# Experts in an order worked out on the chip: by fours at 64 rows, by eights at 32

## The reference

```python
N_GROUPS, EXPERTS_PER_GROUP, TOP_E, D_EXPERT = 4, 8, 2, 512        # 32 experts
def hier_moe(h, wr_g, br_g, wr_e, br_e, w_gate, w_up, w_down):
    p_group = softmax(xf @ wr_g + br_g)
    p_top, g_sel = top_k(p_group, 1)                               # one group of eight
    fine = (xf @ wr_e + br_e)[of that group]
    e_val, e_sel = top_k(fine, 2)                                  # two experts in it
    gate = p_top * softmax(e_val)
    ...
        return (silu(xb @ w_gate[e]) * (xb @ w_up[e])) @ w_down[e] # 1024->512, 1024->512, 512->1024
    out[token] += gate * that
```

## Time and profile before

| | |
|---|---|
| median of three runs | 2012.52 us (2011.01 to 2013.88) |
| span of the profiled execution | 2011.5 us (its own time is not listed apart from the three) |
| PE busy | 1958.3 us, 97% |
| DVE busy | 1026.8 us, 51% |
| first expert stage, router's logits to first addition of its result | 861 to 1331 us |
| second expert stage, the same | 1531 to 1998 us |
| transfers | 593 MB, mean 295 GB/s |

### The profile page before, as it was taken

The page is one execution under the profiler, slowest core; times in us unless marked ns, Lnnn a source line. Parts: engine busy times, 40 slices in busy tenths (PEclk is TensorE's granted clock), DMA queues, the critical chain, the costliest instruction groups (busy, mean ns, idle before and its releaser), DMA issues.

```text
span 2011.5 us, 21703 instructions
## 1 busy us (share of the span) xinstructions
PE 1958.3 (97%) x8110; PEld 1084.0 (54%) x8110; DVE 1026.8 (51%) x1940; ACT 375.6 (19%) x783; POOL 122.8 (6%) x217
## 2 busy tenths in 40 slices
PE   8999999999999999899999999989999999999997
PEld 5557666545776658454444434447865444344442
DVE  3356875445597669686668796743444111011102
ACT  2421001033110000131111111112332211111111
POOL 1121210011121100000000000000000000000000
PEclk9999999999999999899999999999999999999999
DMA  7437876334587751669999999973254999999995
GB/s 264 154 126 256 303 288 251 132 126 167 204 285 287 279 209 43 254 265 408 426 428 427 427 426 427 427 294 126 84 196 173 408 428 427 426 427 427 425 428 235
DMA packets 113351, 593.14 MB, mean 295 GB/s; under 512 B 17767, under 2 KB 22374, under 8 KB 85990
## 3 DMA queue, kind: packets, MB, share of 16 engines
q1 hardware_dynamic: 99430, 541.48, 67.0%
q0 software_dynamic: 13824, 50.34, 7.1%
HBM read 590.74 MB, written 1.05 MB: 294 GB/s over the span
## 4 chain that ended last, share of the span: by engine, by line
PE 87%; DVE 7%; issue 2%; DMA 1%; POOL 1%; ACT 1%; DVEq 0%; SPq 0%; POOLq 0%; ACTq 0%
PE bank L1251 28%; PE bank L897 11%; PE bank L910 10%; PE bank L1124 7%; PE bank L829 6%; PE bank L1226 5%; PE bank L1242 4%; DVE work L2689 3%; PE bank L1034 3%; PE bank L1144 3%; PE bank L943 1%; PE bank L1394 1%; DMA ring<-in_moe_w_up 1%; PE bank L1234 1%; POOL rstd L749 1%
## 5 line engine op out<-in xcount | busy, mean ns | idle before, releaser
L1251 PE MATMUL bank<-ring,work 128*64 128x512 f32 x2240 | 632.7, 593 | 1.5 <-DMA ring<-in_moe_w_up 1.5
L1251 PEld LDWEIGHTS bank<-ring,work 128*64 128x64 f32 x2240 | 202.1, 137 | 311.5 <-issue 311.4
L2689 DVE SCALAR_TENSOR_TENSOR work<-work 128x512 f32<-128x512 f32 x384 | 262.0, 746 | 6.7 <-DVE work L2687 5.3
L897 PE MATMUL bank<-hT,ring 128*128 128x256 f32 x1024 | 225.1, 379 | 0.7 <-ACT hT L1551 0.7
L897 PEld LDWEIGHTS bank<-hT,ring 128*128 128x128 f32 x1024 | 194.4, 190 | 36.9 <-issue 11.7
L2699 DVE SCALAR_TENSOR_TENSOR work<-work,bank 128x512 f32<-128x512 f32 x32 | 22.0, 687 | 355.1 <-ACT work L1756 355.1
L1251 PE MATMUL bank<-seventh,work 128*64 128x512 f32 x384 | 169.1, 593 | 0.0
L1251 PE MATMUL bank<-work 128*64 128x512 f32 x312 | 140.3, 594 | 0.0
L1124 PE MATMUL bank<-hT,ring 128*128 128x256 f32 x608 | 137.9, 389 | 0.6 <-ACT hT L1666 0.6
L829 PE MATMUL bank<-ring,hT 128*128 128x512 f32 (+1 forms) x320 | 135.0, 579 | 0.0
L1124 PEld LDWEIGHTS bank<-hT,ring 128*128 128x128 f32 x608 | 117.9, 195 | 19.7 <-issue 3.2
(11 more groups left out here) (408 smaller groups left out, 2096.8 us busy)
## 6 DMA issues: line engine op xcount, KB each, us to landing
ring<-in_moe_w_gate SPq DMA_DIRECT2D x51, 2048.0 KB, 16.5
ring<-in_moe_w_down SPq DMA_DIRECT2D x44, 2048.0 KB, 19.8
ring<-in_moe_w_up SPq DMA_DIRECT2D x43, 2048.0 KB, 18.7
ring<-in_w_down SPq DMA_DIRECT2D x16, 2048.0 KB, 11.7
ring<-in_w_up SPq DMA_DIRECT2D x16, 2048.0 KB, 10.6
xn<-in_ada_w POOLq DMA_DIRECT2D x48, 512.0 KB, 6.4
work<-in_ada_w POOLq DMA_DIRECT2D x48, 512.0 KB, 7.4
ring<-in_w_in SPq DMA_DIRECT2D x10, 2048.0 KB, 8.1
```

The lines of the kernel that those rows point to most:

```text
L897: last = pe.matmul(b[:, (c % 2) * S:(c % 2) * S + S], w[:, k, c * P:c * P + P], hT[:, k, :], start=(k == 0), stop=(k == DT - 1))
L1251: last = pe.matmul(b[h, :], x[:, k, h], rows_of(i, j + e, k)[:, c0:c0 + 512], start=(k == 0), stop=(k == kk - 1))
L2689: mo.do(dve.scalar_tensor_tensor(fl(bias[:, h]), mask_b, rbt[:, bass.ds(12 * bk + h, 1)], fl(bias[:, h]), ALU.mult, ALU.add))
```

## The change

The order of the experts is worked out on the chip. Places 0 to 3 (`FIXED`) hold experts 0 to 3. Of experts 4 to 31 those with more than 32 tokens come first, then the others, each in their numbers' order. Places 0 to 15 (`HEAVY`) are done as before, in pairs at 64 rows. Places 16 to 31 are done four to a "pair", at 32 rows each (`LIGHT`), eight to a quad: there are 8 + 4 = 12 pairs and 6 quads. If more than 16 places are heavy, four passes are made.

A light pair's units are g, g, g, g, u, u, u, u, d, d, d, d. VectorE moves the ranks and gates into the new order (`rk_at`, `gg_at`) and writes the list of experts as integers (`order_i`). SyncE waits for `order_ready` and loads the number of each expert from place 4 on, when it comes to its gate matrix, and takes the source address of its three transfers from it. The last four units are split in halves, all first halves ahead of all second ones. The bias steps are spread over six quads instead of eight. The scratch for descriptors of POOL's transfers is given as 4096 bytes of a partition (it was not given before; the default is 16384).

```diff
+FIXED, HEAVY, LIGHT = 4, 16, 32
-        UNITS = 6 * (NE // 2)
-        WIDE_QUADS = 5
-        WIDE = 12 * WIDE_QUADS
-        NARROW = tuple(RING_OF[0][(WIDE + x) % 8] for x in range(8) if RING_OF[0][(WIDE + x) % 8] != 8)
+        UNITS = 3 * NE
+        HEAVY_PAIRS, HEAVY_UNITS = HEAVY // 2, 3 * HEAVY
+        PAIRS = HEAVY_PAIRS + (NE - HEAVY) // 4
+        QUADS = PAIRS // 2
+        WIDE = 60
+        NARROW = (5, 0, 1, 2, 3, 4, 6)
...
+            def moe_src(i, j):
+
+                e = place_of(j)
+                if e < FIXED:
+                    return moe_w[kind_of(j)][i, e]
+                if kind_of(j) == 0:
+                    sp.wait_ge(sM["order_ready"], i + 1)
+                    expert_at[e] = sp.value_load(order_i[i][0:1, e:e + 1], min_val=0, max_val=NE - 1)
+                src = moe_w[kind_of(j)][i]
+                return src[bass.ds(expert_at[e], 1), :, :, :].rearrange("e p k n -> (e p) k n")
...
+            def moe_second_halves(i):
+
+                for j in range(UNITS - 4, UNITS):
+                    rows = SLOT[slot_of(i, j)][0].rearrange("p (k n) -> p k n", k=4)
+                    sp.dma_start(rows[:, 2:4, :], moe_src(i, j)[:, 2:4, :]).then_inc(landed2[i], 16)
...
-                def product(b, x, j, k, kk, c0):
-
-                    for e in range(2):
-                        h = slice(SLOTS * e, SLOTS * e + SLOTS)
-                        last = pe.matmul(b[h, :], x[:, k, h], rows_of(i, j + e, k)[:, c0:c0 + 512], start=(k == 0), stop=(k == kk - 1))
+                def product(b, x, p, kind, k, kk, c0):
+
+                    ne, width, unit = shape_of(p)
+                    for e in range(ne):
+                        h = slice(width * e, width * e + width)
+                        last = pe.matmul(b[h, :], x[:, k, h], rows_of(i, unit + ne * kind + e, k)[:, c0:c0 + 512], start=(k == 0), stop=(k == kk - 1))
                     return last
...
                 do(dve.tensor_scalar(slotp, slot_no[:, :], 1.0, None, ALU.add))
+                do(dve.tensor_scalar(slotp_l, slot_no[:, 0:LIGHT], 1.0, None, ALU.add))
                 do(dve.tensor_copy(bcmp, bno))
+                do(dve.memset(over[:, 0:FIXED], 0.5))
...
                 do(dve.tensor_reduce(passes_f[:, 0:1], B(4)[:, 0:NE], AX_X, ALU.max))
+                do(dve.tensor_scalar(over[:, FIXED:NE], B(4)[:, FIXED:NE], float(LIGHT), 0.5, ALU.is_gt, ALU.mult))
...
-                do(dve.tensor_reduce(passes_f[:, 4:5], passes_f[:, 1:4], AX_X, ALU.add))
-                wait()
-                dve.tensor_scalar(passes_i[i][:, :], passes_f[0:1, 4:5], 1.0, None, ALU.add).then_inc(m["passes_ready"], 1)
+                do(dve.tensor_tensor_scan(count_up, over, over, 0.0, ALU.add, ALU.add))
+                wait()
+                do(dve.tensor_scalar(passes_f[:, 4:5], count_up[:, NE - 1:NE], float(HEAVY), 3.0, ALU.is_gt, ALU.mult))
+                wait()
+                do(dve.tensor_reduce(passes_f[:, 5:6], passes_f[:, 1:5], AX_X, ALU.add))
+                wait()
+                do(dve.tensor_scalar(passes_f[:, 6:7], passes_f[:, 5:6], 1.0, 4.0, ALU.add, ALU.min))
+                wait()
+                dve.tensor_copy(passes_i[i][:, :], passes_f[0:1, 6:7]).then_inc(m["passes_ready"], 1)
...
                 do(dve.tensor_tensor(gg[:, :, :], oh1[:, :, :], oh2[:, :, :], ALU.add))
-                wait()
+
+                do(dve.scalar_tensor_tensor(place_f, bcmp, count_up[:, NE - 1:NE], count_up, ALU.add, ALU.subtract))
+                wait()
+                do(dve.scalar_tensor_tensor(place, count_up, -1.0, place_f, ALU.add, ALU.subtract))
+                wait()
+                do(dve.scalar_tensor_tensor(place, over, 2.0, place, ALU.mult, ALU.mult))
+                wait()
+                do(dve.tensor_tensor(place, place, place_f, ALU.add))
+                wait()
+                do(dve.tensor_copy(rk_at[:, :, 0:FIXED], rk[:, :, 0:FIXED]))
+                do(dve.tensor_copy(gg_at[:, :, 0:FIXED], gg[:, :, 0:FIXED]))
+
+                def moved(dst, src):
+                    do(dve.tensor_tensor(perm_x, perm_eq, spread(src, 1, 14), ALU.mult))
+                    wait()
+                    do(dve.tensor_reduce(dst, perm_x, AX_X, ALU.add))
+                    wait()
+
+                for c in range(FIXED, NE, 14):
+                    do(dve.tensor_tensor(perm_eq, spread(place, 1, 14), spread(bcmp[:, c:c + 14], 2, NE), ALU.is_equal))
+                    wait()
+                    moved(order_f[:, c:c + 14], bcmp)
+                    for t in range(TT):
+                        moved(rk_at[:, t, c:c + 14], rk[:, t, :])
+                        moved(gg_at[:, t, c:c + 14], gg[:, t, :])
+                dve.tensor_copy(order_i[i][:, FIXED:NE], order_f[0:1, FIXED:NE]).then_inc(m["order_ready"], 1)
                 dve.wait_ge(m["passes_ready"], i + 1)
...
-                        with dve.Fori(0, WIDE_QUADS) as qd:
+                        with dve.Fori(0, heavy - 1) as qd:
                             quad(it0 + qd, qd, first + qd * MCHAIN, True, low_heads(6 * qd))
-                        def five():
-                            bias_of(6 * WIDE_QUADS, 0, 16)
+                        def to_high():
                             masked_in(8, 12)
                             mo.wait()
-                            bias_of(0, 0, 4, 8, 4)
-
-                        quad(it0 + 5, 5, first + 5 * MCHAIN, True, [five] + high_heads(0, (4, 8, 20, 32, 36, 40)))
-                        quad(it0 + 6, 6, first + 6 * MCHAIN, True, high_heads(10, (0, 8, 12, 22, 32, 38, 44)))
-                        quad(it0 + 7, 7, first + 7 * MCHAIN, False, high_heads(21, (0, 12, 16, 26, 36, 40, 44)))
+                            bias_of(0, 0, 12, 8, 4)
+
+                        quad(it0 + 3, 3, first + 3 * MCHAIN, True, low_heads(18), next_light=True)
+                        quad(it0 + 4, 4, first + 4 * MCHAIN, True,
+                             [lambda: bias_of(24, 0, 32), lambda: bias_of(24, 32, 64), to_high] + high_heads(3, (0, 16, 32, 44)), light=True, next_light=True)
+                        quad(it0 + 5, 5, first + 5 * MCHAIN, False, high_heads(14, (0, 12, 24, 36, 48, 60, 72)), light=True)
...
-    nc = bacc.Bacc("TRN2", target_bir_lowering=False, num_devices=1)
+    nc = bacc.Bacc("TRN2", target_bir_lowering=False, num_devices=1, dynamic_dma_scratch_size=4096)
```

More of the change, by code:

```diff
@@ L393, in first_and_second_block @@
         passes_f = region(7720, 8)
+        over = region(7728, NE)
+        slotp_l = region(7760, LIGHT)
+        perm_eq = zz[:, 0:14 * NE].rearrange("p (j e) -> p j e", j=14)
+        perm_x = mask_b[:, 0:14 * NE].rearrange("p (j e) -> p j e", j=14)
+        rk_at, gg_at = fm, fx
+        count_up, place, place_f = fk[:, 1, :], sel_e[:, 0, :], sel_e[:, 1, :]
+        order_f = fk[:, 0, :]
         mu_var = region(7296, 512)
@@ L454, in rows_of @@
         def rows_of(i, j, k):
-            kk = 4 if j % 6 >= 4 else DT
+            kk = 4 if kind_of(j) == 2 else DT
             parts = SLOT[slot_of(i, j)]
@@ L1269, in hidden @@
                                 pe.wait_ge(m["xt_drained"], 4 * it + 1 + k // 2)
-                            last = product(b, x, unit + 2 * c, k, DT, 0)
+                            last = product(b, x, p, c, k, DT, 0)
                         last.then_inc(m[name], 1)
@@ L1282, in hidden_turned, with down, last_down @@
                     last.then_inc(m["at_filled"], 1)
-                def down(q, pr, unit, hf):
+                def down(q, pr, p, hf):
                     if hf == 0:
                         pe.wait_ge(m["at_drained"], pr + 1)
-                        units_landed(unit + 4, q)
+                        units_landed(p, 2, q)
                     for k in range(4):
-                        last = product((G, U)[hf], aTe, unit + 4, k, 4, 512 * hf)
+                        last = product((G, U)[hf], aTe, p, 2, k, 4, 512 * hf)
                     last.then_inc(m["y_filled"], 1)
-                def last_down(q, pr, unit):
+                def last_down(q, pr, p):
                     pe.wait_ge(m["at_drained"], pr + 1)
-                    units_landed(unit + 4, q)
+                    units_landed(p, 2, q)
                     for half in range(2):
                         if half == 1:
-                            for e in range(2):
-                                pe.wait_ge(*second_half_landed(i, unit + 4 + e, q, before))
+                            pe.wait_ge(*second_halves_landed(i, q))
                         for hf in range(2):
                             for k in (2 * half, 2 * half + 1):
-                                last = product((G, U)[hf], aTe, unit + 4, k, 4, 512 * hf)
+                                last = product((G, U)[hf], aTe, p, 2, k, 4, 512 * hf)
                             if half == 1:
@@ L1339, in quad @@
                                 pe.wait_ge(m["xt_drained"], 4 * it + 3 + hf)
-                            down(q, pr, unit, hf)
```

(9 more changed lines are left out.)

78 lines of the change are left out of this document (44 added, 34 removed).

## The result

The changed kernel took 2039.34 us (median of four runs, 2038.3 to 2041.41) against 2012.99 in the runs beside it: ratio 1.0132, 95% interval 1.0118 to 1.0147, 26.4 us slower. The profiled execution was 2041.41 us long with a span of 2039.7, 28.2 more than the span of before.

A forecast was written before the change was run, and what follows sets the result against it. TensorE and the weight stream were taken to be at their limit together. First layer 17.1 + 13.4 - 6.5 = +24.0, second 0.6 + 0.5 - 6.4 = -5.3, so +18.7 on 2011.5: forecast 2031 us, range 2002 to 2051.

The forecast's parts named there:

- What bounds it: Both expert stages: TensorE and the weight stream are at their limit together; a faster TensorE wins only the stage ends.
- The first rival: Whole stage: TensorE was the bound, saving 114 us a layer, about 1785 us; chance 0.01.
- The order: VectorE behind the first pick: 15.9 us of order work; up product 13.6 us later in the first layer, second layer nothing.
- The numbers: SyncE's expert-number loads: 1.0 us before the first layer's first transfer, 0.5 us in the second layer.
- the other loads lie behind a queue that still has work: SyncE: the other 27 number loads of a layer are covered by queued transfers, except at the next hole.
- The hole before unit 62: First layer: unit 62 waits for the first light group's down product; stream stands 13.4 us (9.6 to 17.2).
- VectorE's way to `upped(8)`: First light group, first layer: gated picks, bias steps, gate and up, reaching 1151.0 in the clock of before.
- Later light groups have three units queued: First layer: three units, 14.7 us, cover a product of 7 to 10 us, so no hole.
- the third rival: Light groups: bursts outlast their cover, products take 13.8 us, 0.8 us at each of nine groups; 2055 us; chance 0.10.
- The ends: Behind each stage's last landing: 6.0 us remain (4.7 all warm, 8.6 cold), gaining 6.5 and 6.4 us.
- The sum: First layer +24.0 us, second layer -5.3, together +18.7 on the span of 2011.5: 2031.2 us.
- Only the ends count: Rival: the stream loses nothing and 12 us are won at the ends, 2000 us; chance 0.14.

The follow-up runs named there:

- the first experiment: Changed kernel with, in the first layer, the sixteen steps that move ranks and gates put behind the first up product's step on VectorE: 2039.57 us, ratio 1.0121.
- The second experiment: Changed kernel with, in the first layer, 24 of 64 bias steps moved behind the first light group's up product on VectorE: 2035.2 us, ratio 1.0110.
- fifth: Changed kernel without the order: place e holds expert e, weights at fixed addresses, no number loaded: 2019.56 us, ratio 1.0035.
- sixth: Changed kernel with the order worked out but fixed weight addresses, so SyncE neither waits for the list nor loads numbers: 2034.86 us, ratio 1.0101.
- eighth experiment: The first experiment's kernel with the 48 bias steps of the first layer's first quad moved to the last quad: 2021.33 us, ratio 1.0048.
- ninth: Eighth experiment's kernel plus the second experiment's bias edit and, first layer only, second halves of units 92 to 94 ahead of unit 95: 2014.54 us, ratio 1.0004.
- tenth: Fifth experiment's kernel plus the second experiment's bias edit and, first layer only, second halves of units 92 to 94 ahead of unit 95: 2013.33 us, ratio 1.0000.
- the last experiment: Ninth experiment's kernel plus three unread products in the second layer, and in the first two second halves instead of three ahead of unit 95: 2011.65 us, ratio 0.9990.
- the kernel with the unread products: Ninth experiment's kernel plus three unread products before the second layer's last wait; in the first layer's last down product, three experts precede the fourth: 2014.16 us, ratio 1.0009.

## Why the prediction was right, point by point

*What bounds it.* Right. Outside the holes both stages ran at 414 to 437 GB/s in stretches of 10 us, but for the edges of a hole (396 behind the first one), 393 from 1600 to 1610, and the dip that the kernel before has too (338 in the first stage, 316 in the second, where it had 339 and 334); TensorE's new waiting cost nothing where the stream ran on. The first rival (TensorE was the bound) is out: TensorE's busy time fell by 181 us, and none of it came back as time.

*The order.* Right in size: 871.82 (first small step) to 887.54 is 15.7 us, 15.9 forecast; a step of 448 elements takes 0.62 and 0.655 with its wait, as interpolated. The up product's step came 14.4 - 1.4 = 13.0 us later, forecast 13.6. From there to TensorE's next product it took 2.0 us longer than before (to 917.89 from 903.73, to 901.46 from 889.33), with a granted clock of 0.57 between 900 and 910, forecast 2.5. The next load came 17.4 - 1.4 = 16.0 later, forecast 17.1 with the number. On the chip the order steps cost 15.3 us. What the prediction did not see is that moving the chain alone wins nothing: the first experiment took most of it out of that path, and the hole came one pair later, since VectorE had no room in the whole first quad. With room there, the kernel with order and numbers is within 1.8 us of the one with neither.

*The numbers.* Right for the first one, too low for the rest. Forecast 1.0 and 0.5, measured 4.5 for both layers, uncertain by some 3 us. The first number cost 1.0, as forecast. The step that failed is "the other loads lie behind a queue that still has work": where two gate loads follow each other on a dry queue the second one pays 0.8 as well, and in the second layer the numbers cost 1.0 to 2.3 us of stream. That makes 2.8 to 4.1 together; where the rest of the 4.5 lies, if it is more than scatter, is open.

*The hole before unit 62.* Right in kind, too large: 8.5 us for 13.4 (its own terms add up to 14.2 less 1.0, so 13.2), below its own lower bound of 9.6. The term that was mis-sized is VectorE's way to `upped(8)`, forecast at 1151.0 + 16.1 = 1167.1, measured 1162.21: picks began 1.8 us earlier, the 16 of them took 3.4 instead of 4.0, and eight bias steps took 5.95 in straight code (1120.46 follows 1114.51) instead of 6.2 in the loop. The bound had been drawn round the clock of TensorE and not round these. The second experiment also shows that 3.4 of the 8.5 remain without VectorE.

*A third hole.* Not in the prediction. "Later light groups have three units queued" leaves out the last group: unit 95 takes the slot of an up matrix of that same group, and ahead of it only three half units are queued, 7.4 us of stream, against an up product that ran from 1327.05 to 1336.51, at a clock of 0.50 for its first four microseconds. 6.1 us of hole; 5.3 came back when three more halves were put ahead. It is the third rival's mechanism (a burst outlasts its cover), in one place and not in nine: the other light bursts took 7.1 to 9.9 us, four tiles side by side, so that rival's 13.8 us for tiles two by two did not come.

*The ends.* Too good in this execution. From the last wait to the first addition it is 7.7 us in both layers (1353.18 to 1360.84, 2018.75 to 2026.43), forecast 6.0, since both bursts ran cold: 6.57 and 6.58 us where 3.5 was hoped for. The reason given (the first halves run directly before) failed: TensorE had finished them and stood for 7.9 us in the first layer and for 4.4 in the second (busy 0.36 of the four from 2014 to 2018), and the clock was at 0.50 from 2018 on. The first layer's burst is slow in every kernel with this end, 5.16 to 6.57 us. The second layer's is not. In five other kernels whose products at this end are the same (first, second, fifth, sixth and eighth experiment) TensorE stood for 1.8 to 2.9 us, the burst ran at a clock of 1.00, and the end took 4.7 us, the warm bound of the forecast; in the ninth and tenth it stood for 3.6 and 2.9 us and the burst took 5.3. The row of the first experiment and that of the ninth:

```profile
2023.56 3.64 PE bank L1288 x32
...
1994.11 5.33 PE bank L1290 x32
```

The Trainium skill, "TensorE: Matmul & The Clock Gate", HAM oscillation, describes bursts that start at the slow clock behind a DMA wait; the two bursts of the kernel after agree with it, the five others did not slow down. The gain in the second layer was also measured from too early a point: 74 GB/s between 1985 and 1990 are bytes that were still landing after the 1985.9 that was taken as the end. So the second layer brought 0.8 us instead of 5.3 in this execution, and 2.6 to 4.5 in the four other kernels whose second layer is the same (440.4 to 442.3 us).

*The sum.* First stage, measured: 16.0 + 8.5 + 6.1, less 12.5 - 7.7 = 4.8, gives 25.8 of the 28.1 us; the other 2.3 were not followed up. Forecast 24.0. The direction and the size held, but partly because a hole too large stood for one that was missing: 13.4 forecast against 8.5 + 6.1. On the span the forecast was 9.5 us too low: 4.1 in the first stage, 4.5 in the second, and 1.4 by which the first slot came free later, less 0.6 between the stages. On the median it is 8.1, as the profiled execution was a long one.

*Only the ends count.* The rival with 0.14 is out as a forecast, and the tenth and the last experiment say more: with most of the holes closed the kernel is 0 to 2.5 us faster than before, not 12.

## What to carry to other kernels

When both a queue and an engine look full, cost the change in time that the queue stands still, and look for the stretch whose other engine has no room: here a computation moved within that stretch only moved the hole, and it had to trade places with work that could go to another stretch. Check each ring's last units by themselves, since the cover there is made of half units and of the slots of the same group. A faster engine in front of a saturated stream wins only the end behind the last landing, and it can lose part of that when it has to wait there and comes back at the low clock.

## What the runs showed of the hardware that was not expected

- A tile of 32 columns alone takes as long as four side by side: eight fp32 products of one expert, 16 records, about 7.0 us at a clock of 1.00, as the 64 records of four take 7.09. The Trainium skill, "TensorEngine Tiling (Array Packing)", Overview, under Theoretical Speedup, gives up to 4x for dimensions of 32 and below; the rows agree for four tiles that run together, and say that nothing is left of it for one.
- The stream ends raggedly: in its last 4 us (2014 to 2018) the DMA share was 0.41, in the kernel with the unread products 0.47 in its last 3 (1988 to 1991). In the kernel before it was 0.18 between 1985 and 1990. It is in these microseconds that TensorE stands still ahead of the last burst.
- A load of a number from memory by SyncE cost 0.8 to 1.0 us on a dry queue. Where the queue still had transfers nearly all of it was hidden: 28 numbers cost the second layer's stream 1.0 to 2.3 us.
